# Two-layer MoE trunk: experts' rows stored in slot order and gathered per token with adding transfers, in place of adding scatters into DRAM

## The chip, the cores and the metric

The kernel runs on one core of a Trainium2 chip. The metric is the device time of one execution in microseconds. Lower is better.

## The reference

Two transformer layers run over 640 tokens of width 1024: 128 context tokens and 512 latent tokens, with separate conditioning vectors. In each layer an attention mixer adds its result to the residual rows `x`; then comes the mixture of experts, where each token goes to 2 of 16 experts:

```
h = rms_norm(x, norm2_g) * (1 + scale2) + shift2
gates = weights of the top 2 experts of the top group, per token      # (T, 16), two non-zero
a = t @ w_gate[e];  u = t @ w_up[e]                                   # 1024 -> 256
hid = silu(a) * u * gates
y = sum over experts of hid @ w_down[e]                               # 256 -> 1024
x = x + gate2 * y
```

After layer 1, `y_prompt` and `y_sample` are `rms_norm(x, final_norm_g)`. The keys and values of the context tokens are outputs too.

## The kernel before

The 640 tokens are NT = 5 tiles of 128 rows; tile 0 holds the context, tiles 1 to 4 the latents. `x_t[t]` is the resident SBUF tile of residual rows, 128 rows of 1024 floats (512 KB). Every engine has its own program, written out by hand; engines meet only at semaphores, and each one takes its own instructions strictly in order.

The mixture of experts works on slots. Each (token, expert) pair, 1280 in all, gets a slot, sorted by expert; `slots_i` holds the two slot numbers of each token (columns `k * NT + t`). 128 slots make one expert tile. There are at least MIN_ET = 10 and at most N_ET = 18 expert tiles, according to the routing; 29 ran in the two layers of the profiled execution (15 and 14). For the tile i:

- PE transposes the gathered rows (`rows_T`), multiplies by gate and up weights (`gate_up`, L2254 for one expert, L2248/L2249 for two), transposes the hidden rows (`hidden_T`) and multiplies by the down weights (`down`, L2296 or L2289/L2290).
- DVE and ACT form `silu`, and DVE (`y_copy`, L1771) writes the weighted 128 x 1024 result to `y_out[i % 2]` and raises `y_evac_d`.
- GpSimd (POOL) issues the gather of tile i's input rows (`h_rows` to `hg`, L893) and, three tiles behind, `y_store(i - 3)` (L879): an indirect DMA with an add, which scatters the 128 rows of `y_out` onto the rows of their tokens in the DRAM tensor `x_rows[l]`. Since a token has two slots, every such DMA waits for the landing of the one before it (`s_yout`).
- SP loads the experts' weights (3 MB an expert) through a ring of four slots. Its program alternates between waits for PE to free a slot (L575 gate and up, L579 down) and waits for a landing that it passes on to PE as `gu_loaded` and `dn_loaded` (L600):

```python
for e in range(RING, NE + 2):
    if e < NE:
        gate_up_of(l, e)                                 # waits gu_done of expert e - 4
    pass_on(gu_loaded, l, e - 2, wgu_landed, 32)
    if RING <= e - 1 < NE:
        down_of(l, e - 1)                                # waits dn_done of expert e - 5
    pass_on(dn_loaded, l, e - 2, wd_landed, 16)
```

`x_rows[l]` must hold the residual rows before the first scatter: `x_store` (L845) writes each `x_t[t]` there while the attention's output is added. When all scatters have landed, POOL raises `x_final` and SP loads the five tiles back into `x_t` (`load_x`, L612), raising `s_xin[t]`. ACT then squares tile t (L950 for the next layer, L978 after the last), POOL takes the root (`norm1_root`, L717 and L722), DVE scales (L1218, or L1201 for the output), and PE transposes (L1799) and starts layer 1's input projection (L1907). After layer 1, SP stores each scaled tile as an output (L670).

Beside this, two stretches that the change touches: at the start of layer 0 POOL issues loads and fills and takes the roots of tiles 2 to 4 in between (`norm1_root(l, t)`, in the loop over t at L764); and near 470 us, in layer 0, SP loads the next layer's `w_mod` columns (L603) just before the first experts' weights, while PE waits to multiply them (L1824).

## Time and profile before

| | |
|---|---|
| three runs | 1403.48, 1405.07, 1409.73 us; median 1405.07 us |
| the profiled execution | 1402.38 us, its span 1400.6 us |
| PE | 1239.2 us busy, 88% of the span |
| DVE, ACT, POOL | 719.1, 412.7 and 233.3 us busy |
| DMA | 250.48 MB, mean 179 GB/s; queue q0 (POOL's) 63.94 MB, q1 (SP's) 183.26 MB |
| expert tiles, layer 0 | first gather issued at 493.8 us, last result written by DVE at 706.6 us |
| expert tiles, layer 1 | first gather issued at 1177.3 us, last result written by DVE at 1369.6 us |

All times of rows are microseconds from the start of the span, unless marked ns. The difference between the execution's time and its span, 1.8 us, lies outside the program. A busy share says how long an engine computed, not that it set the end; for that the chain of waits is followed back from the last instruction. The DMA share of a stretch is the mean time that the packets of the core's 16 DMA engines took, as a share of the stretch, so share times length is engine time.

### The profile page before, as it was taken

To read this page: it belongs to the slowest core of one execution; us is meant where nothing else is said; L and a number is where in the kernel's file an instruction comes from. 1 tells how busy PE (TensorE), PEld (TensorE's weight loads), DVE (VectorE), ACT (ScalarE), POOL (GpSimd) and SP (SyncE) were. 2 spreads that over 40 slices of the span, in tenths; PEclk is the share of its full clock that TensorE was granted. 3 is DMA by queue.
4 is the path that set the end of the run, shared out by engine and by line. 5 is a ranking of instruction groups with operands and counts; after the bars stand their busy time and mean duration, and the time that the engine had idled before them with its cause. 6 is when DMAs were issued, how large, how long until landed. Compare 5 with 4: busy or idle time off the path is not lost.

```text
span 1400.6 us, 22064 instructions
## 1 busy us (share of the span) xinstructions
PE 1239.2 (88%) x7898; PEld 725.4 (52%) x7898; DVE 719.1 (51%) x1728; ACT 412.7 (29%) x931; POOL 233.3 (17%) x335
## 2 busy tenths in 40 slices
PE   4999999999989869988959999899998993999980
PEld 3455556767756534433435554676666662444330
DVE  0344436777834625553514453567786445455442
ACT  2111145766611201111111111567665110111101
POOL 1220021110121112211111001211111111111212
PEclk9899999999999979999969999999999996999995
DMA  9800188010052887999950005760113344899955
GB/s 346 303 15 1 62 302 240 17 47 17 16 177 80 318 358 262 351 375 358 312 174 14 1 1 180 271 153 16 48 31 97 130 153 167 325 372 367 336 179 181
DMA packets 75625, 250.48 MB, mean 179 GB/s; under 512 B 6551, under 2 KB 15392, under 8 KB 62896
## 3 DMA queue, kind: packets, MB, share of 16 engines
q1 hardware_dynamic: 56080, 183.26, 35.1%
q0 software_dynamic: 18976, 63.94, 15.9%
q8 instruction: 99, 1.62, 0.5%
q10 hardware_dynamic: 432, 1.36, 0.2%
q14 instruction: 38, 0.31, 0.1%
HBM read 219.12 MB, written 31.08 MB: 179 GB/s over the span
## 4 chain that ended last, share of the span: by engine, by line
PE 63%; DMA 20%; DVE 7%; issue 6%; DVEq 1%; ACT 1%; POOL 1%; SPq 0%; POOLq 0%; ACTq 0%
PE ps L1907 17%; DMA x_rows<-arena,idx 13%; PE ps L2098 10%; PE ps L1799 8%; PE ps L1981 8%; PE ps L2254 5%; PE ps L2034 5%; PE ps L1824 2%; PE ps L2296 2%; PE ps L2248 2%; DVE ring L1362 2%; DMA ring<-in_w_mod 2%; DMA ring<-in_w_in 1%; DMA x<-in_x_sample 1%; DMA hT_region<-h_rows,idx 1%
## 5 line engine op out<-in xcount | busy, mean ns | idle before, releaser
L1907 PE MATMUL ps<-ring,hT_region 128*128 128x512 f32 (+1 forms) x640 | 270.3, 578 | 3.4 <-ACT hT_region L990 3.4
L1907 PEld LDWEIGHTS ps<-ring,hT_region 128*128 128x128 f32 x640 | 120.9, 192 | 134.4 <-issue 133.9
L1362 DVE TENSOR_SCALAR_CACHE_REDUCE ring<-ps 128x768 f32<-128x768 f32 (+1 forms) x168 | 132.7, 820 | 95.5 <-PE ps L1981 77.6
L1044 ACT ACTIVATE ring<-ring,negm 128x768 f32<-128x768 f32 (+1 forms) x168 | 137.6, 820 | 26.8 <-DVE ring L1362 26.8
L2098 PE MATMUL ps<-ring,hT_region 128*128 128x384 f32 (+1 forms) x480 | 143.5, 454 | 0.0
L2254 PE MATMUL ps<-ring,hT_region 128*128 x272 | 127.2, 623 | 10.3 <-SPq L600 4.3
L1981 PE MATMUL ps<-arena,qT 64*128 64x384 f32 (+1 forms) x640 | 124.8, 507 | 8.5 <-DVE ring L1362 4.1
L2098 PEld LDWEIGHTS ps<-ring,hT_region 128*128 128x128 f32 x480 | 89.2, 190 | 42.9 <-issue 1.5
L2034 PE MATMUL ps<-work,arena 128*64 128x128 f32 x1600 | 105.0, 278 | 5.6 <-ACT work L1060 4.3
L1060 ACT ACTIVATE work<-ps 128x512 f32<-128x512 f32 x128 | 75.8, 592 | 89.1 <-PE ps L1799 89.1
L2034 PEld LDWEIGHTS ps<-work,arena 128*64 128x64 f32 x1600 | 85.9, 136 | 24.6 <-issue 14.3
L2248 PE MATMUL ps<-ring,hT_region 128*64 x192 | 88.2, 614 | 9.8 <-SPq L600 9.8
L879 POOL DMA_INDIRECT x_rows<-arena,idx x29 | 47.9, 1652 | 293.9 <-DVE arena L1771 205.1
L2254 PEld LDWEIGHTS ps<-ring,hT_region 128*128 128x128 f32 x272 | 53.4, 199 | 80.6 <-issue 80.6
L1149 ACT ACTIVATE work<-ps 128x256 f32<-128x256 f32 x29 | 11.2, 384 | 281.8 <-PE ps L2254 158.9
L1758 DVE COPY work<-ps 128x256 f32<-128x256 f32 x29 | 12.3, 424 | 158.9 <-PE ps L1799 158.9
L2249 PE MATMUL ps<-ring,hT_region 128*64 128x512 f32 x192 | 88.3, 614 | 0.0
L1799 PE MATMUL ps<-ident,ring 128*128 128x128 f32 x600 | 81.9, 278 | 0.3
L1799 PEld LDWEIGHTS ps<-ident,ring 128*128 128x128 f32 x600 | 65.2, 140 | 28.0 <-issue 25.1
L1981 PEld LDWEIGHTS ps<-arena,qT 64*128 64x128 f32 (+1 forms) x640 | 56.1, 185 | 41.7 <-issue 15.0
L1237 DVE TENSOR_TENSOR work<-ps,rope 128x256 f32<-128x256 f32 (+2 forms) x40 | 14.0, 350 | 114.4 <-PE ps L1907 113.5
L1824 PE MATMUL ps<-ring,silu_c 128*2 128x128 f32 x1536 | 51.0, 290 | 19.9 <-DMA ring<-in_w_mod 19.2
(305 smaller groups left out, 1724.3 us busy)
## 6 DMA issues: line engine op xcount, KB each, us to landing
ring<-in_w_mod SPq DMA_DIRECT2D x24, 2048.0 KB, 10.5
ring<-in_moe_w_gate SPq DMA_DIRECT2D x32, 1024.0 KB, 11.6
ring<-in_moe_w_up SPq DMA_DIRECT2D x32, 1024.0 KB, 15.2
arena<-in_moe_w_down SPq DMA_DIRECT2D x32, 1024.0 KB, 14.3
ring<-in_w_in SPq DMA_DIRECT2D x6, 2048.0 KB, 20.2
arena<-mod_rows POOLq DMA_DIRECT2D x12, 512.0 KB, 5.7
arena<-fac_rows POOLq DMA_DIRECT2D x20, 256.0 KB, 4.4
x_rows<-x POOLq DMA_DIRECT2D x10, 512.0 KB, 3.1
```

Of the source, the lines that this page charges most:

```text
L1044: act.activation(v, v, ACT.Exp, bias=negm[:, 2 * (k % 3) + m:2 * (k % 3) + m + 1], scale=-1.0, accum_out=sums[:, c:c + 1]).then_inc(exp_do ...
L1060: act.activation(to[:, 512 * b:512 * (b + 1)], ps[:, 4 + b, :], ACT.Copy).then_inc(pt_evac[b], 1)
L1362: ts(o_, i_, -pair_of(p)[4], None, ALU.mult, ALU.min, accum_out=col).then_inc(m_ready, 1)
L1799: return pe.transpose(out, in_, ident[:])
L1824: last = mm(ps[32 * h:32 * h + 2, mod_bank(j), mod_cols(j)], silu_v[:, :, c], w[:, c, 128 * h:128 * (h + 1)], start=(c == 0), stop=(c == K ...
L1907: last = mm(ps[:, b, 0:n], hT[:, c, t * P:(t + 1) * P], w[:, c, :], start=(c == 0), stop=(c == KC - 1))
L1981: last = mm(ps[:, 2 * m + c, 0:384], q[r:r + n, :], kT[r:r + n, plane, 384 * c:384 * (c + 1)], start=True, stop=True)
L2034: last = mm(ps[64 * m:64 * (m + 1), 7, (u % 4) * P:(u % 4 + 1) * P], V[:, s_, vc:vc + 64], w[:, 768 * m + c * P:768 * m + (c + 1) * P], st ...
L2098: last = mm(ps[:, n % 4, 0:w_], oT[:, c, t * P:(t + 1) * P], w[:, c, :], start=(c == 0), stop=(c == KC - 1))
L2248: mm(g[0:HALF], h[:, c, 0:HALF], wa[:, c, :], start=(c == 0), stop=(c == KC - 1))
L2249: last = mm(g[HALF:P], h[:, c, HALF:P], wb[:, c, :], start=(c == 0), stop=(c == KC - 1))
L2254: last = mm(g, h[:, c, :], wa[:, c, :], start=(c == 0), stop=(c == KC - 1))
```

## The change

The DRAM tensors `x_rows` are gone, and with them `x_store`, SP's `load_x` and the semaphore `x_final`. In their place stands a DRAM tensor `y_rows[l]` with one row for each slot (18 x 128 rows).

- `y_store(i)` is a plain DMA of `y_out[i % 2]` to rows i * 128 onward of `y_rows[l]`; it waits for `y_evac_d` alone.
- `x_t[t]` stays in SBUF through the experts' stage. After the last store has landed, POOL issues ten indirect DMAs (`rows_back(t, k)`): for tile t and choice k, the rows of `y_rows[l]` at the slots `slots_i` are gathered and added onto `x_t[t]` in SBUF. The second of a tile waits for the landing of the first. The ten stand in a written order, with the roots of tiles 0 and 1 between them.
- After the last layer the final roots follow the same order (`final_root`).
- At the start, four DMAs of 512 rows (2 MB) each, from `x_sample`, fill the rows 1280 to 2303 of both `y_rows`. They are issued in POOL's queue in layer 0, ahead of `norm1_root(0, 2)`.

```diff
--- before.py
+++ after.py
@@ -168,7 +168,7 @@
     mod_rows = scratch("mod_rows", (DEPTH, 2, 6 * D))
     h_rows = scratch("h_rows", (P + NT * P, D))
     fac_rows = scratch("fac_rows", (DEPTH, NT, 16, P))
-    x_rows = [scratch(f"x_rows{l}", (P + NT * P, D)) for l in range(DEPTH)]
+    y_rows = [scratch(f"y_rows{l}", (N_ET * P, D)) for l in range(DEPTH)]
 
     ctx = ExitStack()
     with ctx:
@@ -368,9 +368,7 @@
         s_hout = sem("s_hout")
         s_hg = [[sem(f"s_hg{l}_{s}") for s in range(2)] for l in range(DEPTH)]
         s_yout = [[sem(f"s_yout{l}_{s}") for s in range(2)] for l in range(DEPTH)]
-        s_xout = sem("s_xout")
         s_xin = [sem(f"s_xin{t}") for t in range(NT)]
-        x_final = sem("x_final")
         s_once = sem("s_once")
         s_yleft = sem("s_yleft")
 
@@ -606,11 +604,6 @@
             def block_in(l, b, to, landed):
                 columns("w_in", l, *BLK[b], to, landed)
 
-            def load_x(l, tiles):
-
-                for t in tiles:
-                    sp.dma_start(x_t[t], x_rows[l][(1 + t) * P:(2 + t) * P, :]).then_inc(s_xin[t], 16)
-
             for g, (kind, l, i, at) in enumerate(USES):
                 to = slot[at]
                 if kind == "moe":
@@ -642,8 +635,6 @@
                     for k, b in enumerate(IN_ORDER):
                         sp.wait_ge(gu_done[l - 1], steps_of(l - 1, NE - RING + k))
                         block_in(l, b, slot[b], w_landed[b])
-                    sp.wait_ge(x_final, l)
-                    load_x(l - 1, range(NT))
                     continue
                 if USE_BEFORE[g] is not None:
                     slot_free(g)
@@ -663,8 +654,6 @@
                 else:
                     columns("w_mod", l, i * 512, (i + 1) * 512, to, w_landed[at])
 
-            sp.wait_ge(x_final, DEPTH)
-            load_x(DEPTH - 1, range(NT))
             for t in range(NT):
                 sp.wait_ge(f_out, t + 1)
                 sp.dma_start(o["y_prompt"][0] if t == 0 else o["y_sample"][0, (t - 1) * P:t * P, :],
@@ -735,6 +724,10 @@
                 dma(V[:, 0:2, 512:768], a["cache_diff_v"][0, l].rearrange("(b p) h n -> p b (h n)", p=P)
                     ).then_inc(s_vcache, 16)
 
+            def final_root(t):
+                pool.wait_ge(ss1_ready, DEPTH * NT + t + 1)
+                rsqrt(rsf[:, t:t + 1], ssf[:, t:t + 1], 1).then_inc(rs1_ready, 1)
+
             def norm1_root(l, t):
                 pool.wait_ge(ss1_ready, l * NT + t + 1)
                 rsqrt(rs1[:, t:t + 1], ss1[:, t:t + 1], 1).then_inc(rs1_ready, 1)
@@ -748,8 +741,7 @@
             dma(x[:, D:].rearrange("p (t n) -> p t n", t=NT - 1),
                 a["x_sample"][0].rearrange("(t p) n -> p t n", p=P)).then_inc(s_setup_dma, 16)
             norm1_root(0, 1)
-            for rows_ in (h_rows, *x_rows):
-                dma(rows_[0:P, :], a["x_prompt"][0]).then_inc(s_once, 16)
+            dma(h_rows[0:P, :], a["x_prompt"][0]).then_inc(s_once, 16)
             dma(lane_w[0:N_ET, :], row_b(a["step_tables"].rearrange("k m e -> (k m e)"), N_TAB * 2 * NE, N_ET)
                 ).then_inc(s_once, 16)
             small_load(pool, 0, 2)
@@ -760,8 +752,13 @@
                     dma(mod_rows[l, k], a["b_mod"][l]).then_inc(s_once, 16)
             for l in range(DEPTH):
                 if l == 0:
-                    pool.wait_ge(s_once, 128)
+                    pool.wait_ge(s_once, 96)
                 for t in range(NT):
+                    if l == 0 and t == 2:
+                        spare = a["x_sample"][0]
+                        for rows_ in y_rows:
+                            for r in range(MIN_ET * P, N_ET * P, T_LAT):
+                                dma(rows_[r:r + T_LAT, :], spare).then_inc(s_once, 16)
                     if t >= 2:
                         norm1_root(l, t)
                     if t >= 1:
@@ -840,10 +837,6 @@
                     pool.wait_ge(h2_ready, l * NT + t + 1)
                     dma(h_rows[(1 + t) * P:(2 + t) * P, :], h2).then_inc(s_hout, 16)
 
-                def x_store(t):
-                    pool.wait_ge(xo_done, l * 15 + 3 * t + 3)
-                    dma(x_rows[l][(1 + t) * P:(2 + t) * P, :], x_t[t]).then_inc(s_xout, 16)
-
                 for t in range(NT):
                     if t >= 1:
                         h2_store(t - 1)
@@ -852,12 +845,10 @@
                         rsqrt(rs2[:, t:t + 1], ss2[:, t:t + 1], 1, ss2b).then_inc(rs2_ready, 1)
                         break
                     rsqrt(rs2[:, t:t + 1], ss2[:, t:t + 1], 1).then_inc(rs2_ready, 1)
-                    x_store(t)
                     if t == 1:
                         factors_out(NT - 1)
                     if t == 2:
                         factors_in(NT - 1)
-                x_store(NT - 1)
                 h2_store(NT - 1)
 
                 pool.wait_ge(idx_ready, l + 1)
@@ -865,21 +856,21 @@
 
                 if l == 0:
 
-                    pool.wait_ge(s_once, 128)
+                    pool.wait_ge(s_once, 160)
 
                 def y_store(i):
 
                     with if_used(pool, i):
                         pool.wait_ge(y_evac_d[l], i + 1)
-                        if i == 0:
-                            pool.wait_ge(s_xout, (l + 1) * 16 * NT)
-                        else:
-
-                            pool.wait_ge(s_yout[l][(i - 1) % 2], 16 * ((i - 1) // 2 + 1))
-                        pool.indirect_dma_start(
-                            out=x_rows[l], out_offset=bass.IndirectOffsetOnAxis(ap=idx[:, i:i + 1], axis=0),
-                            in_=y_out[i % 2], in_offset=None, compute_op=ALU.add
-                        ).then_inc(s_yout[l][i % 2], 16)
+                        dma(y_rows[l][i * P:(i + 1) * P, :], y_out[i % 2]).then_inc(s_yout[l][i % 2], 16)
+
+                def rows_back(t, k):
+                    if k == 1:
+                        pool.wait_ge(s_xin[t], 32 * l + 16)
+                    pool.indirect_dma_start(
+                        out=x_t[t], out_offset=None, in_=y_rows[l],
+                        in_offset=bass.IndirectOffsetOnAxis(ap=slots_i[:, k * NT + t:k * NT + t + 1], axis=0),
+                        compute_op=ALU.add).then_inc(s_xin[t], 16)
 
                 for i in range(N_ET):
                     if i == 2:
@@ -908,16 +899,25 @@
                 for i in range(MIN_ET - 2, N_ET):
                     with if_used(pool, i):
                         pool.wait_ge(s_yout[l][i % 2], 16 * (i // 2 + 1))
-                pool.sem_inc(x_final, 1)
+                def next_root(t):
+                    if l + 1 < DEPTH:
+                        norm1_root(l + 1, t)
+                    else:
+                        final_root(t)
+
+                for t, k in ((0, 0), (1, 0), (2, 0), (0, 1), (1, 1), (3, 0), (2, 1), (4, 0)):
+                    rows_back(t, k)
+                next_root(0)
+                rows_back(3, 1)
+                next_root(1)
+                rows_back(4, 1)
                 if l + 1 < DEPTH:
-                    norm1_root(l + 1, 0)
-                    norm1_root(l + 1, 1)
                     value_loads(l + 1)
-
-            for t in range(NT):
-                pool.wait_ge(ss1_ready, DEPTH * NT + t + 1)
-                rsqrt(rsf[:, t:t + 1], ssf[:, t:t + 1], 1).then_inc(rs1_ready, 1)
-            pool.wait_ge(s_once, 144)
+                else:
+                    for t in range(2, NT):
+                        final_root(t)
+
+            pool.wait_ge(s_once, 176)
             pool.wait_ge(s_ctxout, DEPTH * 96)
 
 
@@ -940,7 +940,7 @@
             def norm1_sums(l, t):
 
                 if l >= 1:
-                    act.wait_ge(s_xin[t], 16 * l)
+                    act.wait_ge(s_xin[t], 32 * l)
                 elif t == 0:
                     act.wait_ge(s_x0, 16)
                 else:
@@ -974,7 +974,7 @@
                 mod_copy(0, j)
 
             def final_sums(t):
-                act.wait_ge(s_xin[t], 16 * DEPTH)
+                act.wait_ge(s_xin[t], 32 * DEPTH)
                 act.activation(work[:, 1024 * (t % 2):1024 * (t % 2 + 1)], x_t[t], ACT.Square, scale=D ** -0.5,
                                accum_out=ssf[:, t:t + 1]).then_inc(ss1_ready, 1)
                 act.drain()
@@ -1196,7 +1196,7 @@
 
             def final_scale(t):
 
-                dve.wait_ge(s_once, 144)
+                dve.wait_ge(s_once, 176)
                 dve.wait_ge(rs1_ready, DEPTH * NT + t + 1)
                 stt(x_t[t], x_t[t], rsf[:, t:t + 1], gain_f, ALU.mult, ALU.mult).then_inc(f_out, 1)
 
@@ -1494,7 +1494,7 @@
 
                         dve.wait_ge(s_gate1, (l + 1) * 32)
 
-                        dve.wait_ge(s_once, 128)
+                        dve.wait_ge(s_once, 160)
                     dve.wait_ge(wo_done, l * 15 + n + 1)
                     tt(xo_tmp[:, 0:c1 - c0], ps[:, n % 4, 0:c1 - c0], (gate1l if t else gate1c)[:, c0:c1], ALU.mult)
                     dve.drain()
```

## Rows read from the trace of the kernel before

**Rows 1.** The page's chain that ended last, by line

```profile
PE ps L1907 17%; DMA x_rows<-arena,idx 13%; PE ps L2098 10%; PE ps L1799 8%; PE ps L1981 8%; PE ps L2254 5%; PE ps L2034 5%; PE ps L1824 2%; PE ps L2296 2%; PE ps L2248 2%; DVE ring L1362 2%; DMA ring<-in_w_mod 2%; DMA ring<-in_w_in 1%; DMA x<-in_x_sample 1%; DMA hT_region<-h_rows,idx 1%
```

**Rows 2.** DVE's timeline, last result of each layer: start, us, engine, line

```profile
705.18 1.41 DVE L1771 SCALAR_TENSOR_TENSOR arena<-ps,w_slot,qT 128x512 f32<-128x512 f32 x2 [4.57 <-PE ps L2296]
...
1368.14 1.41 DVE L1771 SCALAR_TENSOR_TENSOR arena<-ps,w_slot,work 128x512 f32<-128x512 f32 x2 [4.65 <-PE ps L2296]
```

**Rows 3.** The chain in time, layer 0 into 1: start, us, what

```profile
710.43 6.04 DMA x_rows<-arena,idx
...
722.11 0.25 POOL small L717
```

**Rows 4.** The same chain, end of the kernel

```profile
1370.18 7.25 DMA x_rows<-arena,idx
...
1378.27 0.33 SPq L612
...
1380.65 9.13 DMA x<-x_rows
```

**Rows 5.** PE's waits for SP: layer 0's experts, then layer 1's (total, times, longest)

```profile
PE ps L2248 <- SPq L600: 6.8, 2, 4.0
...
PE ps L2254 <- SPq L600: 2.1, 1, 2.1
...
PE ps L2248 <- SPq L600: 3.0, 1, 3.0
```

**Rows 6.** Windows: length; PE, PEld, DVE, ACT, POOL busy; PEclk, DMA share, GB/s

```profile
1351.30:1357.30 6.00, 4.94 (x16) 2.17 (x16) 1.55 (x3) 1.42 (x2) 1.54 (x1) 1.00 0.56 87
...
1370.20:1377.40 7.20, 0.00 (x0) 0.00 (x0) 0.00 (x0) 0.00 (x0) 1.53 (x1) 0.72 0.50 75
...
1378.30:1389.80 11.50, 0.00 (x0) 0.00 (x0) 3.72 (x3) 4.60 (x8) 3.17 (x6) 0.50 0.88 312
...
1190.00:1196.00 6.00, 5.51 (x28) 2.83 (x27) 0.46 (x1) 0.84 (x2) 0.22 (x1) 1.00 1.01 421
```

**Rows 7.** SP's own waits: from 640 to 650, 614 to 634, 1324 to 1340

```profile
SPq L579 <- PE ps L2290: 14.1, 1, 14.1
...
SPq L600 <- DMA arena<-in_moe_w_down: 5.4, 2, 3.7
...
SPq L600 <- DMA arena<-in_moe_w_down: 2.0, 1, 2.0
```

**Rows 8.** PE's timeline: gate and up of one expert, after a wait and without

```profile
648.27 8.82 PE L2254 MATMUL ps<-ring,hT_region 128*128 x16 [2.15 <-SPq L600]
...
685.59 7.03 PE L2254 MATMUL ps<-ring,hT_region 128*128 x16
```

**Rows 9.** POOL's timeline

```profile
37.89 0.83 POOL L748 DMA_DIRECT2D x<-in_x_sample  x1 [22.64 <-DMA ring<-in_w_in]
...
474.42 0.63 POOL L845 DMA_DIRECT2D x_rows<-x  x1
...
543.98 1.57 POOL L879 DMA_INDIRECT x_rows<-arena,idx  x1 [9.03 <-DVE arena L1771]
...
545.86 0.97 POOL L893 DMA_INDIRECT hT_region<-h_rows,idx  x1 [0.30 <-issue]
```

**Rows 10.** DMA issues of the page: count, KB each, median to landing

```profile
x_rows<-x POOLq DMA_DIRECT2D x10, 512.0 KB, 3.1
```

**Rows 11.** PE's timeline: layer 0's last w_mod

```profile
485.70 3.49 PE L1824 MATMUL ps<-ring,silu_c 128*2 128x128 f32 x64 [2.58 <-DMA ring<-in_w_mod]
```

**Rows 12.** Tile 2 in layer 0 (DVE, PE); the page's DMA slices

```profile
78.84 0.75 DVE L1218 TENSOR_SCALAR work<-x,small 128x1024 f32<-128x1024 f32 x1 [4.65 <-POOL small L722]
...
84.50 0.60 PE L1799 MATMUL ps<-ident,work 128*128 128x128 f32 x4
...
DMA  9800188010052887999950005760113344899955
```

**Rows 13.** The chain again: layer 1's first gather, alone on the DMA engines

```profile
1177.32 4.36 DMA hT_region<-h_rows,idx
```

## The prediction, made before the changed kernel was run

> **What bounds the kernel now.** I read the chain that ended last first. PE's matmuls hold most of it; the largest item that is no computation is the adding scatter into `x_rows`, 13% of the span [rows 1]. That share misleads. The chain runs through scatter after scatter only because each waits for its forerunner, while PE works beside them. To see what the scatters cost I looked at where the last one stands against the last result of the experts. In layer 0, DVE wrote that result at 705.18 + 1.41 = 706.6 [rows 2]; the last scatter was issued at 710.43, because the one before it was late, and landed at 716.5; the root of tile 0 for layer 1 began at 722.11 [rows 3]. In layer 1 the result stood at 1369.6 [rows 2], the scatter took from 1370.18 to 1377.4, the loads of `x` began at 1378.27, and the last of them landed at 1380.65 + 9.13 = 1389.8 [rows 4]; the span ends 10.8 later, at 1400.6. So the removed work is exposed in two places only: 15.5 from the last result to a root that can start (layer 0), and 20.2 from the last result to the last resident tile (end).
>
> Inside the experts' loops the question is what PE waits for. It waits for SP to pass on weights: 6.8 + 2.1 in layer 0, and 3.0 plus one wait like layer 0's 2.1 in layer 1, 14.0 together [rows 5]. The DMA engines are often full there, as in 1190 to 1196 [rows 6], so this looks like bandwidth. SP's own waits say otherwise. Ahead of PE's wait that ends near 648, SP had stood for 14.1 in L579, waiting for PE's down matmuls; it was released by PE, not by a landing [rows 7]. SP's program simply puts a wait for PE in front of a signal whose weights are there. Only ahead of two waits did SP also wait for a landing: up to 3.7 and 2.0 [rows 7]. After such a wait PE also runs slower: 16 matmuls take 8.82 against 7.03 without one [rows 8].
>
> **What an adding transfer costs.** This decides the case. In the stretches where one adding scatter of 512 KB moves nearly alone, the DMA share times the length is 0.56 x 6.0 = 3.4 and 0.50 x 7.2 = 3.6 [rows 6]: 3.5 of the 16 engines' time for each. For plain transfers, the stretch of `x` loads moved 312 GB/s x 11.5 = 3.6 MB in 0.88 x 11.5 = 10.1, so 1.5 for each 512 KB, and at 421 GB/s it is 1.25 [rows 6]. An add costs more than twice a copy. From issue to landing one alone takes 6.0 [rows 3], and issues follow each other by 545.86 - 543.98 = 1.9 [rows 9].
>
> The change's adding gathers have the same two reads and one write for each row of 4 KB, with the added-to row in SBUF instead of DRAM; the trace has none of them. Bounds: 1.9 a transfer, if POOL's issue limits, up to 3.6. I take 3.5, the nearest row; an ALU or the way a packet is handled would be the same for both. The Trainium skill, in "Collectives: The Full Stack", section "Stop ④ — SDMA + CCE: where bytes move and the add happens", describes the adding transfer as read-read-write "with the add free in between". By 3.5 the sum below is +24.5; with an add as cheap as a copy it would be about 0 (third rival). [...]
>
> **The change, step by step.**
>
> 1. End of the kernel. The last store is issued where the scatter was, 1370.1, and lands 3.1 later (a plain 512 KB write of POOL [rows 10]), at 1373.2. The step from landing to next issue took 1378.27 - 1377.43 = 0.85 in before, for the branches of unused tiles [rows 4]; the first adding gather starts at T0 = 1374.1. It lands after 6.0, the other nine follow at 3.5: 1374.1 + 6.0 + 31.5 = 1411.6. POOL's waits inside the order do not add to that, since two or three transfers are queued whenever it waits. Against 1389.8 [rows 4] that is **+21.8**. With issues as the limit: three issues to T0 + 3.8, the fourth after the first landing (6.0 + 0.5), the eighth at 14.1, landed at 20.1, the tenth issued at 20.6 and landed at 26.6: 1400.7, +10.9. What follows the last landing (square, root, scale, store; 10.8) stays.
>
> 2. From layer 0 to layer 1. The result stands at 706.6 [rows 2]; the store is issued at 707.1, free of the 3.4 that the scatter waited for its forerunner, and lands at 710.2; T0 = 711.0. Tile 0 needs the first and the fourth transfer: 711.0 + 6.0 + 3 x 3.5 = 727.5, the square 1.25, so its root can begin at 728.8. POOL is ready just then: it must first issue the eight transfers ahead of the root, the seventh of which waits for the third landing (T0 + 13.0), so it is free near 728.3. Against 722.11 [rows 3]: **+6.7**. With issues as the limit POOL is free at T0 + 16 = 727.0: +4.9. Behind the waiting POOL stand the root of tile 1, which waits for the landing of the sixth transfer (T0 + 23.5), and the value loads; both are covered by PE's projection of tile 0, of which DVE needs the root only near the end. The five loads of `x` in SP's queue go; nothing waited behind them.
>
> 3. In the loops. 29 adding scatters become plain stores: some 3.5 - 1.25 = 2.25 less DMA time each, and no wait for a forerunner in POOL's queue, so the gathers behind it go out no later. PE was not waiting for these gathers. Of PE's 14.0 only the part behind landings can come back: at most 3.7 + 2.0, plus the slower clock after it, 8.82 - 7.03 = 1.8 each. I take **-3.0**, between 0 and -9.
>
> 4. The five `x_store` of a layer. POOL issues them (0.63 each) and stands idle behind them; nothing there is late. The last of layer 0 goes out at 474.42 [rows 9], beside the `w_mod` load for which PE waits 2.58 until 485.70 [rows 11]: 512 KB less in a saturated stretch is 1.25 [rows 6]. **-1.0**, between 0 and -1.25. In layer 1 no load is waited for there: 0.
>
> 5. The fill. Four DMAs of 2 MB at about 78, ahead of tile 2's root. A 2 MB load took 0.83 to issue [rows 9]: 3.3. DVE's scale of tile 2 ran 78.84 to 79.6, and its transposes began at 84.50 [rows 12]: 4.9 of slack, so 0. Were each issue as long as an adding scatter's, 1.57 [rows 9], it would be 6.3 - 4.9 = +1.4. The bytes themselves, 16 times 512 KB, need 16 x 3.5 = 56 at the worst, and the DMA slices are empty from 70 to 175 [rows 12].
>
> Sum: 21.8 + 6.7 - 3.0 - 1.0 = +24.5. The profiled execution took 1402.4 (span 1400.6 and 1.8 outside), which gives 1426.9. The median of the runs is 2.7 higher, 1405.1, and the same step gives **1429.6**.
>
> **The rivals.**
>
> - *POOL's issue is the limit, not the engines.* The isolated scatters' 3.5 could hold latency of DRAM's second read, which queued transfers into SBUF hide. Then the ends cost 10.9 + 4.9: 15.8 - 4.0 = +11.8, **1416.9**; a price between 1.9 and 3.5 falls between this and the forecast. For: each engine has a queue of packets at the tails, where it had but one transfer. Against: alone on the engines, an adding transfer lands 6.0 after its issue and a plain one 3.1 [rows 3, 10], and the longer issue, 1.57 against 0.63 [rows 9], explains only 0.9 of the 2.9; the other 2.0 on top of 1.25 is again some 3.2 of moving.
> - *PE's waits in the loops were bandwidth after all.* Then all 14.0 return, and four slowed stretches of 1.8, together 21.2: 28.5 - 21.2 - 1.0 = +6.3, **1411.4**. It decides where weights land before SP stands in L579. Against: SP stood 14.1 for PE [rows 7].
> - *The other side: the add is free.* Ten transfers cost as plain gathers: landing 4.4 after issue [rows 13], issues each 0.97 + 0.30 = 1.27 apart [rows 9]. The eighth issue is at T0 + 10.0, landed 14.4, the tenth lands at T0 + 19.3 = 1393.4, +3.6; POOL reaches the root at T0 + 11.3, +0.2; in all 3.8 - 4.0, about 0: **1405**. Between 1.9 a transfer (ends 15.8) and 1.27 (ends 3.8) the 11.0 that would leave the kernel within 7.0 of before lies at 1.65: from there down it is not slower. For: nothing in the trace. Against: 3.4 and 3.6 for each adding scatter [rows 6]. [...]
>
> **How the numbers follow.** Forecast 0.54; issue limit or a price between 0.25; loops 0.07; add free 0.09; anything worse (fill exposed, no gain in the loops) 0.05. The predicted time is the forecast's. The range goes up to 1405.1 + 22.7 + 7.0 + 1.4, about 1437 (3.6 a transfer, no gain in the loops), and down to 1410, just below the second rival; it leaves out the free add and the corners. 0.5%, about what a measurement of this kernel can tell from no change, is 7.0: the free add and most of the second rival lie within it, 0.13; faster needs two rivals at once, 0.05; slower 0.82.
>
> **What would show it.** After the last DVE L1771 of each layer, a landing about 3 later, then ten transfers of which the landings follow at 3.5 (right), 1.9 (first rival) or under (third); a stretch of DMA share near 1.0 at some 150 GB/s at the end. The root of tile 0 in layer 1 starts 6 to 7 later after the last result than before. PE's waits for SP L600 near 2 remain in the loops; if they are gone, the second rival holds. PE's wait for `w_mod` shrinks by about one. The prediction is wrong if the span from the last result to the end is not about 52 against 31 before.

## The result and the profile after

Timed side by side, the changed kernel took 1416.35 us (median of four runs, 1415.30 to 1420.63) and the kernel before 1404.28 us (four runs, 1403.30 to 1409.73): ratio 1.0085, 95% interval 1.0061 to 1.0109. That is 12.1 us slower; 24.5 were forecast. A second timing of the unchanged file gave 1420.00 and 1.0097 (1.0074 to 1.0120), 14.1 above the kernel before. Of all executions two were in a slow state and are left out of the ratios: one of plain_sums below (2961.26) and one of the kernel before (1546.77). The profiled execution took 1415.30, its span 1413.5, 12.9 more than before's 1400.6.

The page's chain that ended last, by line, which answers to [rows 1]:

```profile
PE ps L1907 17%; PE ps L2098 10%; PE ps L1799 8%; PE ps L1981 8%; PE ps L2254 5%; PE ps L2034 5%; DMA x<-y_rows,slots_i 3%; PE ps L1824 2%; PE ps L2296 2%; PE ps L2248 2%; DVE ring L1362 2%; DMA ring<-in_w_in 1%; DMA x<-in_x_sample 1%; DMA ring<-in_w_mod 1%; DMA hT_region<-h_rows,idx 1%
```

The scatters' 13% have gone, 3% for the gathers back have come, and the kernel is slower. The share of the scatters was mostly time in which PE worked beside them.

DVE's timeline after the change, the last result of each layer, as in [rows 2]:

```profile
698.30 1.41 DVE L1771 SCALAR_TENSOR_TENSOR arena<-ps,w_slot,qT 128x512 f32<-128x512 f32 x2 [4.56 <-PE ps L2296]
...
1363.49 1.41 DVE L1771 SCALAR_TENSOR_TENSOR arena<-ps,w_slot,work 128x512 f32<-128x512 f32 x2 [4.57 <-PE ps L2296]
```

The results stand at 699.7 and 1364.9, 6.9 and 4.7 earlier than before. What follows them takes longer. The chain in time from layer 0 into layer 1, as in [rows 3]: the last store, two of the adding gathers, the root of tile 0.

```profile
700.00 3.00 DMA y_rows<-arena
...
704.33 6.31 DMA x<-y_rows,slots_i
...
711.08 9.23 DMA x<-y_rows,slots_i
...
721.58 0.25 POOL small L706
```

The same chain at the end of the kernel, as in [rows 4]; the last line is the square of the last tile:

```profile
1365.20 2.97 DMA y_rows<-arena
...
1369.64 1.66 POOL x L870
...
1385.27 11.22 DMA x<-y_rows,slots_i
...
1396.89 6.58 DMA x<-y_rows,slots_i
...
1403.49 1.06 ACT work L978
```

From the last result to the root of tile 0 it is 721.58 - 699.7 = 21.9 against 15.5; from the last result to the last landing 1403.47 - 1364.9 = 38.6 against 20.2 to 20.3. The window over the first nine gathers of the end answers to the scatter's windows [rows 6], in the same columns:

```profile
1369.60:1396.50 26.90, 0.00 (x0) 0.00 (x0) 2.57 (x2) 3.45 (x6) 15.74 (x13) 0.50 0.96 188
```

The DMA engines are full (0.96) while 188 GB/s move; full of plain loads they moved 421 [rows 6]. (One output store of 512 KB is among the bytes of this window.)

The whole difference, from the two profiles:

| stretch | before | after | difference | forecast |
|---|---|---|---|---|
| start to layer 0's first gather | 493.8 | 492.0 | -1.8 | -1.0 |
| layer 0, first gather to last result | 212.8 | 207.7 | -5.1 | -3.0 for both layers |
| last result to root of tile 0 | 15.5 | 21.9 | +6.4 | +6.7 |
| that root to layer 1's first gather | 455.2 | 454.9 | -0.3 | 0 |
| layer 1, first gather to last result | 192.2 | 188.4 | -3.8 | (above) |
| last result to last landing | 20.3 | 38.6 | +18.3 | +21.8 |
| last landing to the end | 10.8 | 10.0 | -0.8 | 0 |
| sum | 1400.6 | 1413.5 | +12.9 | +24.5 |

One pair of profiles isn't the whole story. A second profile of the changed kernel (after_again below) has a span of 1420.3, 6.8 more (it is of the slowest of its six runs), and 4.5 of that lie in layer 0's loop, which took 212.2 there, nearly as long as before the change. The mean granted clock of that loop, third from the right in these windows, differs: before the change, then the changed kernel's first and second profile.

```profile
493.80:706.60 212.80, 186.38 (x670) 81.97 (x670) 99.77 (x156) 30.28 (x45) 38.48 (x30) 0.94 0.93 335
```

```profile
492.01:699.71 207.70, 183.32 (x664) 81.06 (x664) 98.71 (x148) 30.28 (x45) 23.14 (x30) 0.95 0.88 344
```

```profile
492.57:704.81 212.24, 187.34 (x664) 82.10 (x664) 98.79 (x146) 30.27 (x45) 23.21 (x30) 0.93 0.87 338
```

PE's waits for SP after the change (total, times, longest), layer 0's experts and then layer 1's, as in [rows 5]:

```profile
PE ps L2248 <- SPq L598: 5.2, 2, 2.8
PE ps L2254 <- SPq L598: 2.2, 1, 2.2
...
PE ps L2254 <- SPq L598: 2.1, 1, 2.1
PE ps L2248 <- SPq L598: 1.0, 1, 1.0
```

All five waits are still there. Only two are shorter: in layer 0 the one of 4.0 (of 6.8 in two waits 5.2 are left), in layer 1 the one of 3.0. Those are the two ahead of which SP had also waited for a landing [rows 7].

### The profile page after: what moved, and what is told of

The parts are those of the page before. It is cut to its first block, busy times and chain, and to the rows that moved or that the text cites. A ratio compares the mean times of both kernels' runs of the same rounds, so it can differ in the third digit from the quotient of the medians.

```text
span 1413.5 us, 22035 instructions
## 1 busy us (share of the span) xinstructions
PE 1233.1 (87%) x7898; PEld 723.8 (51%) x7898; DVE 718.4 (51%) x1728; ACT 412.7 (29%) x931; POOL 227.4 (16%) x347
## 4 chain that ended last, share of the span: by engine, by line
PE 62%; issue 17%; DMA 9%; DVE 7%; POOL 2%; DVEq 1%; ACT 1%; POOLq 0%; SPq 0%; ACTq 0%
PE ps L1907 17%; PE ps L2098 10%; PE ps L1799 8%; PE ps L1981 8%; PE ps L2254 5%; PE ps L2034 5%; DMA x<-y_rows,slots_i 3%; PE ps L1824 2%; PE ps L2296 2%; PE ps L2248 2%; DVE ring L1362 2%; DMA ring<-in_w_in 1%; DMA x<-in_x_sample 1%; DMA ring<-in_w_mod 1%; DMA hT_region<-h_rows,idx 1%
## 5 line engine op out<-in xcount | busy, mean ns | idle before, releaser
L2254 PE MATMUL ps<-ring,hT_region 128*128 x272 | 126.1, 618 | 10.2 <-SPq L598 4.3
L2248 PE MATMUL ps<-ring,hT_region 128*64 x192 | 84.8, 595 | 6.2 <-SPq L598 6.2
L2249 PE MATMUL ps<-ring,hT_region 128*64 128x512 f32 x192 | 84.9, 595 | 0.0
L1799 PEld LDWEIGHTS ps<-ident,ring 128*128 128x128 f32 x600 | 65.2, 140 | 28.0 <-issue 25.1
L2296 PE MATMUL ps<-arena,work 128*128 x136 | 66.2, 632 | 2.4 <-DVE work L1758 2.4
L865 POOL DMA_DIRECT2D y_rows<-arena x29 | 16.1, 555 | 311.1 <-DVE arena L1771 297.3
## 6 DMA issues: line engine op xcount, KB each, us to landing
ring<-in_moe_w_up SPq DMA_DIRECT2D x32, 1024.0 KB, 12.6
```

Source lines behind the costliest of these rows:

```text
L1799: return pe.transpose(out, in_, ident[:])
L2248: mm(g[0:HALF], h[:, c, 0:HALF], wa[:, c, :], start=(c == 0), stop=(c == KC - 1))
L2249: last = mm(g[HALF:P], h[:, c, HALF:P], wb[:, c, :], start=(c == 0), stop=(c == KC - 1))
L2254: last = mm(g, h[:, c, :], wa[:, c, :], start=(c == 0), stop=(c == KC - 1))
L2296: last = mm(ps[:, 5 + k, :], h[:, c, :], wa[:, c, k * 512:(k + 1) * 512], start=(c == 0), stop=(c == 1))
```

## The experiments

Each is one edit of the changed kernel or of the kernel before. The expectations were written before the runs. Where an edit is long, only its main lines are shown, with "..." for what is left out. end_plain, scatter_plain and stores_adding leave layer 1's sums out or wrong; they serve for the time alone.

**end_plain**: the last layer's gathers back without their add.

```diff
-                        compute_op=ALU.add).then_inc(s_xin[t], 16)
+                        **({} if l + 1 == DEPTH else {"compute_op": ALU.add})).then_inc(s_xin[t], 16)
```

> The last layer's ten gathers copy instead of adding (so the last layer's sums are left out); POOL's order and waits stay. Theory E (the DMA engines' time for an add sets the end): the landings follow POOL's issues, 1.3 to 1.9 apart, the first lands after 4.4; from the first issue to the last landing about 20 instead of 33.8, kernel about 1416.4 - 13 = 1403. Rival I (POOL's order and its waits set it): the wait of each second gather stays, at least 30 from first issue to last landing, kernel 1412 to 1416.

Measured: 1410.85 (ten runs), ratio 1.0037 (1.0019 to 1.0055). Its chain at the end:

```profile
1376.34 6.03 DMA x<-y_rows,slots_i
...
1387.73 6.50 DMA x<-y_rows,slots_i
...
1394.63 6.25 DMA x<-y_rows,slots_i
```

From the first issue to the last landing it is 1400.88 - 1376.34 = 24.5, against 33.8 with the add: 9.3 less without the add. But the number lies between what the two theories gave, since even plain gathers take over 6 each when others are queued beside them. The last one, with no other gather left, took 6.25 beside output stores: 284 GB/s moved from 1394.6 to 1400.9, more than three times 512 KB. The edit changes the length of an issue (0.94 for 1.54) with the price of moving, so it doesn't part the two. That took add_probe.

**end_order**: the last layer's ten gathers in the order of all first choices, then all second ones, with both roots after them, so that POOL never stands before a landing for long.

```diff
...
+                    for k in range(2):
+                        for t in range(NT):
+                            rows_back(t, k)
+                    next_root(0)
+                    next_root(1)
```

> Only in the last layer, all five first gathers are issued before the five second ones, and the roots come after them, so that POOL hardly waits for a landing. Theory E: the engines were busy nearly all the time anyway; from first issue to last landing 33 instead of 33.8, and the last tile's end unchanged: kernel 1415 to 1416.4. Rival I: the three waits of 2.5, 3.1 and 3.4 in POOL's queue go, -6 to -9: kernel 1408 to 1410.

Measured: 1416.85 (four runs), ratio 1.0069 (1.0042 to 1.0096), which can't be told from the changed kernel. Its chain at the end:

```profile
1374.03 1.66 POOL x L870
...
1381.59 10.53 DMA x<-y_rows,slots_i
...
1392.50 13.40 DMA x<-y_rows,slots_i
```

31.9 from the first issue to the last landing in place of 33.8; seven profiles with the old order gave 33.6 to 35.4. The order is worth 1.9 or little more there, and nothing that the kernel's time shows; ten adding transfers cost over 30 in either order. Theory E's 33 was near, the second theory's 1408 to 1410 is ruled out.

**add_probe**: after the end of the changed kernel, POOL issues 512 KB transfers alone on the chip, each of four kinds in a queue of eight; the two adding kinds also one by one. `out_row` is a store from SBUF to DRAM, `in_row` an indirect gather into SBUF, and `settle` waits for all that was issued.

```diff
+            for j in range(8):
+                out_row(j)
+            settle()
+            for j in range(8):
+                out_row(j, accum_op=ALU.add)
+            settle()
...
+            for j in range(8):
+                in_row(j, compute_op=ALU.add)
+            settle()
...
+            for j in range(8):
+                in_row(j)
+            settle()
```

> The changed kernel, and after its outputs have landed POOL moves 512 KB tiles with nothing beside them: 8 plain stores, 8 adding stores to DRAM at once, 4 adding stores one by one, 8 adding gathers into SBUF at once, 4 one by one, 8 plain gathers. If an add's price is the engines' own, whatever its destination: both queued kinds 2.8 to 3.0 apart, plain ones 1.3 to 1.5. If the destination matters (the forecast's 3.5 was that of DRAM): adding stores 3.5 apart, adding gathers 2.8. If it is queued against alone: both 2.8 apart queued, and DMA share times length 3.5 for one alone.

Measured: windows of the four queues (plain stores, adding stores, adding gathers, plain gathers), columns as in [rows 6]; the last two rows are the chain's, an adding store and an adding gather by itself.

```profile
1412.60:1425.20 12.60, 0.00 (x0) 0.00 (x0) 0.00 (x0) 0.00 (x0) 4.36 (x8) 0.50 0.86 333
1425.60:1448.90 23.30, 0.00 (x0) 0.00 (x0) 0.00 (x0) 0.00 (x0) 7.12 (x8) 0.50 0.95 180
1472.60:1497.70 25.10, 0.00 (x0) 0.00 (x0) 0.00 (x0) 0.00 (x0) 12.46 (x8) 0.50 0.89 167
1524.30:1539.00 14.70, 0.00 (x0) 0.00 (x0) 0.00 (x0) 0.00 (x0) 7.58 (x8) 0.50 0.79 285
```

```profile
1449.12 5.40 DMA probe<-ring
...
1497.94 6.17 DMA ring<-y_rows,slots_i
```

From the first issue to the last landing the adding stores took 23.2, the adding gathers 25.1. Queued, an adding store costs (23.2 - 5.4) / 7 = 2.54 and an adding gather (25.1 - 6.2) / 7 = 2.70, less than the expected 2.8 to 3.5. With 3.0 for one plain store alone (2.97 and 3.00 above) and 4.4 for one plain gather alone [rows 13], the plain queues give (12.6 - 3.0) / 7 = 1.37 and at most (14.7 - 4.4) / 7 = 1.47. So an adding transfer costs nearly twice a copy, and nearly the same into DRAM and into SBUF. It is not POOL's issue: the stores' eight issues took 7.12 busy of 23.3, and the gathers' came every 1.54 + 0.30 = 1.84, less than 2.70. This shows the first rival's mechanism wrong, and the third rival too.

The sentence of the Trainium skill that the prediction quotes ("Collectives: The Full Stack", section "Stop ④ — SDMA + CCE: where bytes move and the add happens") describes a read-read-write "with the add free in between". The runs don't refute it: it calls the addition free and still counts a second read. They show the price of the whole transfer, 2.54 and 2.70 against 1.37 and 1.47, and none parts the second read from the addition. Nor does it speak for the third rival.

**scatter_plain**: the kernel before, with layer 1's scatters not adding; order and waits stay.

```diff
-                            in_=y_out[i % 2], in_offset=None, compute_op=ALU.add
+                            in_=y_out[i % 2], in_offset=None,
+                            **({} if l + 1 == DEPTH else {"compute_op": ALU.add})
```

> The kernel before, with layer 1's scatters writing instead of adding (so that layer's sums are left out); each still waits for its forerunner. It tells what shortened the loops. Theory D (the adds' DMA time): layer 1, from the first gather's issue to the last result, 187.6 instead of 192.2 as in the changed kernel's 188.4, and the last scatter lands 2 sooner; kernel about 1404.3 - 6 = 1398. Rival W (the wait for the forerunner delayed POOL's queue): 192.2 stays, kernel about 1402 (the last scatter alone).

**stores_adding**: the changed kernel, with layer 1's stores adding but free of the wait for the forerunner (the rows they add to are filled at the start).

```diff
...
-                        dma(y_rows[l][i * P:(i + 1) * P, :], y_out[i % 2]).then_inc(s_yout[l][i % 2], 16)
+                        dma(y_rows[l][i * P:(i + 1) * P, :], y_out[i % 2],
+                            **({"accum_op": ALU.add} if l + 1 == DEPTH else {})).then_inc(s_yout[l][i % 2], 16)
```

> The changed kernel with the last layer's stores adding onto their rows of y_rows (first filled; so that layer's sums are wrong), without any wait for a forerunner. Theory D (the adds' DMA time lengthens the loop): layer 1, first gather's issue to last result, 192 as in the kernel before, not 188.4. Rival W (the wait for the forerunner): 188.4 stays.

Measured: scatter_plain 1397.12 (five runs), ratio 0.9942 (0.9919 to 0.9966), layer 1's loop 188.5; stores_adding 1427.39 (one run), its loop 192.7. PE's wait for SP in that loop, first of scatter_plain, then of stores_adding (the line numbers are one higher there than in the other kernels):

```profile
PE ps L2249 <- SPq L600: 1.0, 1, 1.0
```

```profile
PE ps L2249 <- SPq L598: 3.2, 2, 2.7
```

The two kernels hold one half of the change each. Adds gone, waits kept: 188.5. Waits gone, adds kept: 192.7. So layer 1's loop is shorter because the adds' DMA time is gone and one wait for weights shrinks by 2.0; the wait for the forerunner played no part. The windows over that loop, of scatter_plain and of stores_adding, show the DMA share (the column before the last) at 0.81 and 0.88; the changed kernel has 0.81 and the kernel before 0.88 as well.

```profile
1176.53:1365.06 188.53, 172.75 (x636) 76.21 (x636) 93.27 (x147) 28.24 (x42) 27.48 (x29) 0.95 0.81 316
```

```profile
1182.45:1375.15 192.70, 174.56 (x636) 76.92 (x636) 93.33 (x147) 28.26 (x42) 27.58 (x29) 0.94 0.88 309
```

An estimate from these windows: (0.88 x 192.7 - 0.81 x 188.5) / 14 transfers = 1.2 of the engines' time for each add, as 2.54 - 1.37 of add_probe. The rest of the 3.9 is PE at the lower clock behind the longer wait. Before the change the third to fifth pair of matmuls behind the wait of 2.99 took 1.06 each, at a granted clock of 0.50 (1335.8 to 1338.4), and the sixth 0.99; behind the changed kernel's wait of 1.03 they took 0.59 from the second on. The first rows are the kernel before's, the others the changed kernel's:

```profile
1334.91 0.64 PE L2248 MATMUL ps<-ring,hT_region 128*64 x1 [2.99 <-SPq L600]
...
1335.84 1.06 PE L2248 MATMUL ps<-ring,hT_region 128*64 x1
```

```profile
1332.05 0.64 PE L2248 MATMUL ps<-ring,hT_region 128*64 x1 [1.03 <-SPq L598]
1332.52 0.59 PE L2248 MATMUL ps<-ring,hT_region 128*64 x1
```

The time of 1427.39 is no measure of the adds: of the 11.0 above 1416.35, 4.7 lie in layer 0's loop (212.4 against 207.7), where nothing was changed.

**stores_serial**: the changed kernel, with each plain store waiting for the landing of the one before.

```diff
                         pool.wait_ge(y_evac_d[l], i + 1)
+                        if i > 0:
+                            pool.wait_ge(s_yout[l][(i - 1) % 2], 16 * ((i - 1) // 2 + 1))
```

> The changed kernel, with each plain store waiting for the landing of the store before it, as the scatters did. Theory D: the loops stay as short as in the changed kernel (last results at 699.7 and 1364.9, within 1), kernel 1416 to 1417. Rival W: the loops lengthen by 5 and 4, kernel 1424 to 1425.

Measured: 1422.82 (four runs), ratio 1.0114 (1.0078 to 1.0150), an interval that overlaps with both of the changed kernel's. Layer 1's loop took 188.5, which is again no cost of the wait. Layer 0's took 215.1, the longest of all profiles. There PE's matmuls behind a wait for weights ran at half clock. Windows behind that wait, of stores_serial, of the second profile of the changed kernel, and of its first (the column to read is PEclk, the third from the right):

```profile
603.90:605.90 2.00, 1.99 (x6) 0.77 (x8) 0.00 (x0) 0.00 (x0) 0.97 (x1) 0.50 1.06 365
```

```profile
603.50:605.50 2.00, 2.00 (x6) 0.77 (x8) 0.00 (x0) 0.00 (x0) 1.05 (x2) 0.50 0.99 410
```

```profile
601.60:603.60 2.00, 1.97 (x10) 0.80 (x12) 0.00 (x0) 0.00 (x0) 1.08 (x2) 1.00 1.05 377
```

PE's timeline at that place, the first matmul behind the wait, in the changed kernel's second profile and in its first:

```profile
603.49 1.11 PE L2248 MATMUL ps<-ring,hT_region 128*64 x1 [2.76 <-SPq L598]
```

```profile
601.63 0.64 PE L2248 MATMUL ps<-ring,hT_region 128*64 x1 [2.76 <-SPq L598]
```

The same wait of 2.76 was followed by the 1.2 GHz level in one execution and by 2.4 GHz in the other. Such places make layer 0's loop vary: the nine profiles without adding scatters in it or waits between stores gave 206.1 to 212.4, mean 209.7, and the longer ones show the lower mean clock (0.96 for the two shortest, 0.93 for the four longest); the two with adding scatters gave 212.8 and 211.0 at 0.94. So what the change gained in layer 0 isn't settled by these profiles. In layer 1 there is no such spread: ten profiles without adds gave 187.6 to 189.5, mean 188.5, and two with them 192.2 and 192.7. So of stores_serial's 215.1 I can't say how much is the wait and how much the clock.

**after_again and x_writes**: the changed kernel as it is, and with `x_store` put back (into a tensor that nothing reads). x_writes was first run once, then both were timed together.

```diff
...
+                def x_store(t):
+                    pool.wait_ge(xo_done, l * 15 + 3 * t + 3)
+                    dma(x_spare[l][t * P:(1 + t) * P, :], x_t[t]).then_inc(s_xout, 16)
```

> The changed kernel with the five writes of x of each layer put back, into a DRAM tensor that nobody reads. If they delay the w_mod load of layer 0: PE waits 2 to 3 for it again, and the first gather of layer 0 goes out 1 to 2 later than in the changed kernel (492.0), near 493.8; the kernel 1 to 2 longer. If not: 492 stays.

> The changed kernel itself, unaltered, timed again beside the two that follow so that they can be held against it. Its first median was 1416.4, 12.1 above before: the same is expected, 1414 to 1419. Loop of layer 1 from first gather to last result 188.4, as in every kernel here without adding transfers beside it; layer 0's loop anywhere from 206 to 212, since it has varied that much between profiles of like code.

> The changed kernel with the five plain writes of the residual rows put back in each layer (into a DRAM tensor that nothing reads; GpSimd waits for their landing before the gathers back), now timed. Theory W, step 4 of the forecast: the write beside the last w_mod load costs 1.0 in layer 0, so the first gather is issued at 493.8 instead of 492.8 and the time is 1.0 above the changed kernel's. Rival V, these writes cost nothing anywhere: no difference in the first gather's issue and a ratio of 1. One profile of it showed the gather at 491.6, which speaks for V.

Measured: x_writes 1419.46 in its single run; timed, after_again 1420.00 and x_writes 1422.57 (six runs each), ratios 1.0097 (1.0074 to 1.0120) and 1.0124 (1.0101 to 1.0147), which overlap. after_again came out above the expected 1414 to 1419, with loops of 212.2 and 189.5.

Layer 0's first gather was issued at 491.6 in the first profile of x_writes and at 493.76 in the second, against 492.57 in after_again. In the second one PE's wait for `w_mod` was back:

```profile
PE ps L1833 <- DMA ring<-in_w_mod: 1.6, 1, 1.6
```

But it didn't set the gather, which waited for the landing of `h_rows`, and the whole stretch ran 2.0 later from before the `w_mod` matmuls on. Here are those matmuls and the gather, of the first and of the second profile:

```profile
473.46 3.68 PE L1833 MATMUL ps<-ring,silu_c 128*2 128x128 f32 x128
```

```profile
475.50 3.68 PE L1833 MATMUL ps<-ring,silu_c 128*2 128x128 f32 x128
```

```profile
493.76 1.07 POOL L892 DMA_INDIRECT hT_region<-h_rows,idx  x1 [8.97 <-DMA h_rows<-work]
```

From those matmuls to the gather it is 18.1 and 18.3 with the writes put back, 18.5 (after) and 18.4 (after_again) without, and 19.9 in the kernel before. So Theory W isn't borne out, though its 493.8 was met: the writes, put back, lengthen this stretch in neither profile. Over all profiles the first gather came at 493.5 with writes of `x` (four) and at 492.8 without (eight), but each kind spreads over 3, so the 0.7 shows nothing. What shortened the stretch from 19.9 to 18.5 stays open.

**plain_sums**: a version that follows from the above. Plain gathers where the adds cost most: all ten at the end go, plain, into the weight ring, which is free by then, and DVE adds them; of layer 0 only tile 0's two, into the `hg` buffers.

```diff
...
+                def plain_back(t, k):
+                    pool.indirect_dma_start(
+                        out=came_back(l, t, k), out_offset=None, in_=y_rows[l],
+                        in_offset=bass.IndirectOffsetOnAxis(ap=slots_i[:, k * NT + t:k * NT + t + 1], axis=0)
+                    ).then_inc(s_xin[t], 16)
...
+            def add_back(l, t):
+                dve.wait_ge(s_xin[t], 32 * (l + 1))
+                for k in range(2):
+                    last = tt(x_t[t], x_t[t], came_back(l, t, k), ALU.add)
+                    if k == 0:
+                        dve.drain()
+                last.then_inc(x_sum, 1)
...
```

> No add in the DMA where the end waits for it: tile 0 between the layers and all five tiles after the last one are gathered plainly into free SBUF (20 transfers become 12 plain ones and 8 adding ones, the adding ones covered by PE's projection), and DVE adds them onto x, 1.3 an add. Theory E: root of layer 1's tile 0 14 after the last result instead of 21.9, last tile's square about 29 after the last result instead of 38.6; kernel 1416.4 - 8 - 11 = 1397, so below both kernels (1405). Rival I: the issues and the landing of the last store remain, DVE's ten adds come on top: kernel 1410 to 1416.

Measured: 1406.05 (twelve runs), ratio 1.0009 (0.9989 to 1.0028): the same as before, and some ten faster than the changed kernel. Both theories missed: E gave 1397, the other 1410 to 1416. Its chain from layer 0 into layer 1 (gather, two adds, root), and at the end:

```profile
704.65 5.79 DMA hT_region<-y_rows,slots_i
...
710.47 1.23 DVE x L1225
...
711.76 1.24 DVE x L1225
...
714.26 0.25 POOL small L713
```

```profile
1388.12 1.06 ACT work L1003
```

From layer 0's last result (697.9) to the root it is 16.4 (14 expected), against 21.9 with adding gathers and 15.5 before; at the end 1388.12 - 1357.6 = 30.5 (29 expected), against 38.6 and 20.3. The adds by DVE (two of 1.23 a tile) save 8.1 at the end; what is left above before there, 10.2, is what the ten transfers, the adds and the waits between them take where before had one scatter and five loads. The loops' gain pays for that, and no more. The profiled execution, 1400.33, is the fastest of the twelve. No version was run that beats both. Two things weren't measured: layer 0 as in plain_sums with layer 1 as before, and the changed kernel without its fill (no_fill_timed was to show it and gave no time, since the gathers would then be given a tensor with rows that nothing has set).

## Why the prediction was right or wrong

The direction was right and the measured time lay within the range, but the gain and the loss were both mis-sized, and the sum came out at twice what was measured. The steps that failed are two sizes: step 3 put the loops at -3.0, and step 1 priced a queued adding transfer at 3.5.

**Step 3, the loops: the term furthest off in this pair.** Forecast -3.0 within 0 to -9; the pair of profiles shows -5.1 - 3.8 = -8.9, at the end of that range. What the prediction read was right: the structural waits stayed, the two behind landings shrank (3.0 to 1.0 in layer 1, 4.0 to 2.4 in layer 0). The mistake was to take a third of the bound. Layer 1 alone, which repeats within 2 in ten profiles, gives 3.9, of which 2.0 is the wait and the rest the clock behind it; the prediction had both terms (2.0, and 1.8 for the clock), 3.8, and cut them for no reason read from a row. scatter_plain and stores_adding show the cause in layer 1, the adds' DMA time, though each add freed 1.2 of it and not 2.25. In layer 0 the prediction had 3.7 and 1.8, and the wait gave back 1.6. The profile of the result shows 5.1, the second profile 0.6 and the mean over profiles 2.2: part of the 5.1 is how the clock was granted in one execution. By the second profile the loops gave 3.4, near the forecast; how much of the median's miss lies in layer 0 stays open.

**Step 1, the end.** Forecast +21.8, measured +18.3; two errors that partly cancel. The price of a queued adding transfer was taken as 3.5, from share times length of a scatter running alone [rows 6]. Nine gathers were down 1396.49 - 1369.64 = 26.85 after the first issue: 6.3 for the first and (26.85 - 6.3) / 8 = 2.57 for each other one; add_probe has 2.54 and 2.70 by themselves. Nine intervals at 3.5 in place of eight at 2.57 is 10.9 too much. The other error: "POOL's waits inside the order do not add to that". The last gather waits for the one before it on the same tile, was issued at 1396.89 when that had landed, and had no other gather beside it, only output stores: 0.4 + 6.58 = 7.0 that the sum had as one of the nine intervals at 3.5. The window shows them, 239 GB/s:

```profile
1397.00:1403.50 6.50, 0.00 (x0) 0.00 (x0) 2.57 (x2) 1.16 (x3) 3.31 (x5) 0.50 0.95 239
```

With first issue to last landing at 33.8 instead of 37.5, and the first issue 0.2 later after the result than forecast, that is the 3.5 that the term was off. This step is off in every profile: the second gave 39.3 from the last result to the last landing, +19.1. end_order shows that the wait can be avoided for a gain of 1.9 only, since then the others take longer.

**Step 2, the boundary.** Forecast +6.7, measured +6.4. It is right with a price that is wrong: the fourth transfer landed at 720.31, 16.0 after the first issue, for which 6.0 + 3 x 3.5 = 16.5 was written. At 2.57 it should have been 14. It took 9.23 from its own issue, beside four later ones that were issued before it landed. As these rows read, transfers that are queued together share the engines rather than finish in turn, so the one that is waited for pays for those behind it; no run tests that by itself.

**Step 4**: forecast -1.0; 1.8 in the pair, of which 0.3 had come before the `w_mod` matmuls. PE's wait of 2.58 [rows 11] is gone in all eight profiles without the writes, but also in one of the two with the writes put back, and those two have the gather no later after the `w_mod` matmuls than the changed kernel. So the size came out near and the cause given for it isn't shown. **Step 5**: 0 forecast, and the rows show none of it on the path, though no run without the fill gave a time. They are POOL's fill, DVE's scale of tile 2 and PE's last `w_mod` matmuls, which follow without a wait:

```profile
78.00 1.99 POOL L761 DMA_DIRECT2D y_rows<-in_x_sample  x4
```

```profile
80.98 0.75 DVE L1218 TENSOR_SCALAR work<-x,small 128x1024 f32<-128x1024 f32 x1 [6.63 <-POOL small L711]
```

```profile
480.87 5.34 PE L1824 MATMUL ps<-ring,silu_c 128*2 128x128 f32 x128
```

The four issues took 1.99, not 3.3, and DVE's scale came 2.1 later than in [rows 12], inside the 4.9 of slack.

**The rivals.** The first, POOL's issue as the limit, gave 1416.9, the measured time nearly to the number, and is still wrong. Its ends would have cost 15.8; they cost 24.7. It hits by luck, because the loops and the small terms gave back 11.8 where it had 4.0. The second fell: the waits on SP's order stayed, 10.5 of 14.0. The third fell with add_probe and with end_plain's 9.3. The price did lie between, 2.57 ("a price between 1.9 and 3.5 falls between this and the forecast"); the time didn't, since 1416.35 is below this rival's 1416.9 too, because of the loops.

Two smaller things. The range's upper end adds up to 1405.1 + 31.1 = 1436.2, not 1437. And of its own signs: the landings followed at 2.57, not at 3.5; the root came 6.4 later, as said; and the span from the last result to the end was 48.6 (49.3 in the second profile) where it named about 52 against 31, so by that sign the price was too high.

## What to carry to other kernels

A transfer that adds cost the DMA engines nearly twice a copy here, into DRAM and into SBUF (2.54 and 2.70 against 1.37 and 1.47), so look for where it stands: beside a full DMA queue its cost is hidden but for the waits that it stretches, and moved behind the last result every one of them is on the path (38.6 against 20.3 at the end). Where transfers are chained, the chain of waits puts a large share on them that says nothing of their worth; measure from the last result of the stage to the first use of it. A rival whose number fits isn't thereby right: compare term by term before believing it. And compare more than one profile of each kernel before a difference of a few microseconds is put down to the change.

## What was not expected of the hardware

- Share times length of an adding transfer alone (in add_probe 0.65 x 5.4 = 3.5 for a store and 0.54 x 6.2 = 3.3 for a gather) is more than what it takes in a queue: eight adding stores held the engines 0.95 x 23.3 / 8 = 2.8 each, and followed each other by 2.54. So the share of an isolated transfer overstated its price here; that it holds waiting which a queue fills is likely, but not shown.
- The same wait of 2.76 ahead of PE's matmuls was followed by the 2.4 GHz level in one execution and by 1.2 GHz in another of the same kernel. Profiles of like code thus differed by up to 6 over layer 0's loop; the runs don't show what decides it.
- Plain gathers of 512 KB that run beside other transfers took 6.0 to 6.5 to land, against 4.4 for one alone [rows 13]. The last of end_plain's was no cheaper than the first (6.25 and 6.03), since the output stores of the finished tiles ran beside it.
